# One token tile of head 0 scored ahead in an expert-retrieval layer, and two modulation steps moved

## What is computed

```
mod = silu(c) @ w_ada + b_ada                      # 2048 x 12288: sh1, sc1, g1, sh2, sc2, g2
h   = rmsnorm(x) * (1 + sc1) + sh1
sq, sk, sv, cq, ckv, kr = split(h @ w_in)
sb  = stick_breaking_attention(sq, sk, sv)         # 8 heads of 128
q   = rmsnorm(cq) @ w_uq ; kv = rmsnorm(ckv) @ w_ukv   # latents; rope on 64 columns of each head
x   = x + g1 * (concat(rmsnorm(sb), rmsnorm(mla(q, kv))) @ w_o)
h2  = rmsnorm(x) * (1 + sc2) + sh2
q   = h2 @ w_peer_q                                # 8 heads of 2 halves of 128
s1, s2 = q[..., 0, :] @ keys1, q[..., 1, :] @ keys2
16 best of s1, of s2, and of their 256 sums  ->  16 experts and gates for each token and head
y   = sum over 128 experts of gate * gelu(h2 . u[expert]) * v[expert]
out = rmsnorm(x + g2 * y)
```

## Time and profile before

| | |
|---|---|
| median of three runs | 1845.99 us |
| profiled execution | 1844.33 us |
| its span (first to last instruction) | 1841.7 us |
| DMA over the span | 716 MB, 389 GB/s in the mean |
| granted TensorE clock, mean | 0.972 |
| TensorE, VectorE, ScalarE, GpSimd busy | 80%, 62%, 19%, 34% |
| chain that ended last | DMA 58%, VectorE 15%, TensorE 15%, GpSimd 6% |

### The profile page before, as it was taken

How to read it: one execution, slowest core, us unless ns; L and a number is a source line. 1 busy time by engine, 2 the same in 40 slices (tenths; PEclk the granted TensorE clock), 3 DMA queues, 4 the chain that set the end, 5 groups by cost and what they waited for, 6 DMA issues and landing times.

```text
span 1841.7 us, 13707 instructions
## 1 busy us (share of the span) xinstructions
PE 1475.1 (80%) x4834; PEld 828.1 (45%) x4834; DVE 1142.5 (62%) x1562; ACT 350.9 (19%) x697; POOL 620.3 (34%) x625
## 2 busy tenths in 40 slices
PE   2979998899899897777777777777877777777776
PEld 2549986777788633232323323233322323232332
DVE  5858886688789955555555555538555555544445
ACT  3004332663301211010011101101111111010100
POOL 0001111001154773444343443417643443433341
PEclk9889999999999899999999999998999999999999
DMA  9999998459879999999999999999999999999995
GB/s 341 386 389 404 399 354 326 176 187 379 323 303 413 421 421 421 422 422 422 422 421 422 422 422 422 422 421 402 422 422 422 422 422 421 422 422 422 422 422 233
DMA packets 138241, 716.43 MB, mean 389 GB/s; under 512 B 11158, under 2 KB 15436, under 8 KB 63692
## 3 DMA queue, kind: packets, MB, share of 16 engines
q0 software_dynamic: 82976, 604.02, 79.4%
q1 hardware_dynamic: 55212, 111.77, 16.5%
HBM read 713.65 MB, written 2.10 MB: 389 GB/s over the span
## 4 chain that ended last, share of the span: by engine, by line
DMA 58%; DVE 15%; PE 15%; POOL 6%; issue 4%; ACT 1%; SPq 1%; DVEq 0%; POOLq 0%; ACTq 0%
DMA u_rows<-in_peer_u,expert 49%; DVE u_rows L1740 6%; PE ps L768 4%; DMA v_rows<-in_peer_v,expert 4%; DVE first_acc L454 3%; POOL v_rows L665 3%; POOL u_rows L665 3%; PE ps L762 2%; DMA ada_first<-in_w_ada 2%; PE ps L425 2%; DMA ada_late<-in_w_ada 2%; PE ps L927 2%; DVE ada_acc L293 2%; DMA u_rows<-in_peer_v,expert 1%; PE ps L732 1%
## 5 line engine op out<-in xcount | busy, mean ns | idle before, releaser
L1012 PE MATMUL ps<-v_rows,diag 128*128 128x512 f32 x1960 | 905.6, 608 | 269.8 <-DMA v_rows<-in_peer_v,expert 255.6
L1740 DVE SCALAR_TENSOR_TENSOR u_rows<-u_rows,h 128x2048 f32<-128x2048 f32 x256 | 587.1, 2293 | 519.5 <-DMA u_rows<-in_peer_u,expert 514.7
L1012 PEld LDWEIGHTS ps<-v_rows,diag 128*128 128x128 f32 x1960 | 358.8, 191 | 815.2 <-issue 586.5
L665 POOL DMA_INDIRECT u_rows<-in_peer_u,expert x256 | 284.9, 1113 | 621.1 <-DVE u_rows L1740 576.4
L665 POOL DMA_INDIRECT v_rows<-in_peer_v,expert x249 | 287.2, 1153 | 97.0 <-issue 78.6
L1339 ACT ACTIVATE diag<-ident,hidden 128x128 f32<-128x128 f32 x250 | 89.6, 398 | 847.8 <-PE ps L1012 534.2
L293 DVE SCALAR_TENSOR_TENSOR ada_acc<-ada_late,cact,ada_acc 128x2048 f32<-128x2048 f32 x57 | 133.9, 2349 | 19.5 <-DMA ada_late<-in_w_ada 18.5
L279 POOL DMA_DIRECT2D ada_late<-in_w_ada x61 | 32.4, 532 | 321.9 <-DVE ada_acc L293 275.8
L981 PE MATMUL ps<-h2T,ring 128*128 128x256 f32 x512 | 117.7, 390 | 6.4 <-DMA ring<-in_w_peer_q 6.4
L981 PEld LDWEIGHTS ps<-h2T,ring 128*128 128x128 f32 x512 | 99.6, 197 | 20.6 <-DMA ring<-in_w_peer_q 6.8
L454 DVE SCALAR_TENSOR_TENSOR first_acc<-ada_first,cact,first_acc 128x1024 f32<-128x1024 f32 x60 | 77.0, 1284 | 16.9 <-DMA ada_first<-in_w_ada 11.5
(11 more groups left out here) (273 smaller groups left out, 1256.4 us busy)
## 6 DMA issues: line engine op xcount, KB each, us to landing
ada_late<-in_w_ada POOLq DMA_DIRECT2D x61, 1024.0 KB, 7.7
ada_first<-in_w_ada SPq DMA_DIRECT2D x64, 512.0 KB, 11.7
ring<-in_w_in SPq DMA_DIRECT2D x10, 2048.0 KB, 23.5
ring<-in_w_o SPq DMA_DIRECT2D x8, 2048.0 KB, 19.1
ring<-in_w_peer_q SPq DMA_DIRECT2D x8, 2048.0 KB, 14.3
opened<-in_w_in SPq DMA_DIRECT2D x8, 1024.0 KB, 13.0
u_rows<-in_peer_u,expert POOLq DMA_INDIRECT x256, 32.2
v_rows<-in_peer_v,expert POOLq DMA_INDIRECT x249, 34.2
```

The source lines that it names most:

```text
L665: nc.gpsimd.indirect_dma_start(buf[:, :], None, table, bass.IndirectOffsetOnAxis(ap=expert[:, q, k:k + 1], axis=0)).then_inc(done, 16)
L1012: ins = nc.tensor.matmul(ps[:, c, :], diag[i % len(diag)][:, :], buf[:, 512 * c:512 * c + 512], start=(n % HALF_SLOTS == 0), stop=last)
L1740: nc.vector.scalar_tensor_tensor(out=buf[:, :], in0=buf[:, :], scalar=1.0, in1=h2[:, q // H, :], op0=ALU.mult, op1=ALU.mult, accum_out=hid ...
```

## The change

Three edits. First, head 0 is computed with exchanged operands: `h2T` of one token tile is stationary and the head's 256 weight columns move, tile 0 first, and tile 1 behind it in three pieces. The result has tokens on partitions, so it is copied (`q0`), transposed (`p0_t`), copied into `pq`, scored against the keys of head 0 (`sc0_t`) and copied into `s_all`, each for one tile. `retrieve` waits for the scores of its own tile. Second, `ADA_IN` and `ADA_OUT` go from 71 and 86 to 73 and 88: pieces 71 and 72 are summed ahead of attention, and five instead of seven stand behind the norm. `ada_cols(3)` moves ahead of `qpe`, and `ada_finish(3)` with pieces 64 and 65 ahead of the rope. Third, in the output projection `ada_cols(4)` goes from pair (2,5) to (2,1), and two of the 15 places of pieces change.

```diff
     assert e_next[0] + 512 * len(diag) <= 229376
+    q0 = at("q0", e_next[0], [P, TT, 2 * P])
...
-    plan([f"p{u}" for u in range(8)], [0, 1, 2, 3])
-    plan([f"sc{u}" for u in range(8)], [4, 5])
+    plan(["fq_0", "fq_1", "p0_0", "p0_1"] + [f"p{u}" for u in range(1, 8)], [0, 1, 2, 3])
+    plan(["sc0_0", "sc0_1"] + [f"sc{u}" for u in range(1, 8)], [4, 5])
...
-    ADA_IN, ADA_OUT = 71, 86
+    ADA_IN, ADA_OUT = 73, 88
...
                 fill(ins, f"uq{u}")
+            ada_cols(3)
             wr = w.rearrange("p kc (h n) -> p kc h n", h=H)
...
-            ada_cols(3)
             w = group(pe, "w_ukv", 2 * n_in, KVR // P)
...
-                    if n == 2 and m == 5:
+                    if n == 2 and m == 1:
                         ada_cols(4)
...
+            w0 = ring[item["w_pq0"][0]][:, :].rearrange("p (kc n) -> p kc n", kc=KC)
+            def first_head(t, lo, hi):
+                if lo == 0:
+                    take(pe, f"fq_{t}")
+                for ch in range(lo, hi):
+                    if t == 0 and ch % 2 == 0:
+                        copied(pe, f"h2T{ch // 2}")
+                    if t == 0 and ch % KH == 0:
+                        loaded(pe, "w_pq0", ch // KH)
+                    ins = nc.tensor.matmul(ps[:, unit[f"fq_{t}"][0], 0:2 * P], h2T[:, ch, P * t:P * t + P], w0[:, ch, 0:2 * P],
+                                           start=(ch == 0), stop=(ch == KC - 1))
+                if hi == KC:
+                    fill(ins, f"fq_{t}")
+            def first_turned(t):
+                copied(pe, f"fq_{t}")
+                bank = take(pe, f"p0_{t}")
+                for s in range(2):
+                    ins = nc.tensor.transpose(bank[:, P * s:P * s + P], q0[:, t, P * s:P * s + P], ident[:, :])
+                fill(ins, f"p0_{t}")
+            def first_score(t):
+                copied(pe, f"p0_{t}")
+                bank = take(pe, f"sc0_{t}")
+                for s in range(2):
+                    ins = nc.tensor.matmul(bank[:, P * s:P * s + P], pq[:, 0, s, P * t:P * t + P], kT[:, H * s, :], start=True, stop=True)
+                fill(ins, f"sc0_{t}")
+            first_head(0, 0, KC)
+            first_head(1, 0, 3)
+            first_turned(0)
+            first_head(1, 3, 6)
+            first_score(0)
+            first_head(1, 6, KC)
+            token_rows(0)
+            first_turned(1)
+            token_rows(1)
+            first_score(1)
+            token_rows(2)
+            token_rows(3)
-            for u in range(H):
+            for u in range(1, H):
...
-                if u == 0:
-                    token_rows(0)
-                    score(0)
-                    for k in range(1, 4):
-                        token_rows(k)
...
+            first_query(0)
+            first_query_turned(0)
+            first_scores_out(0)
+            first_query(1)
+            token_rows_out(0)
+            first_query_turned(1)
+            token_rows_out(1)
+            first_scores_out(1)
+            token_rows_out(2)
+            token_rows_out(3)
...
             ada_sums(59, 64)
+            ada_finish(3)
+            ada_sums(64, 66)
             for t in range(TT):
                 bank = full(dve, f"qpe{t}").rearrange("p (h n) -> p h n", h=H)
...
-            ada_finish(3)
-            ada_sums(64, ADA_IN)
+            ada_sums(66, ADA_IN)
...
-                    if (n, m) in ((1, 0), (1, 1), (1, 2), (1, 3), (1, 6), (1, 7), (2, 0), (2, 1), (2, 2), (2, 6), (2, 7), (3, 0), (3, 1), (3, 2), (3, 3)):
+                    if (n, m) in ((1, 0), (1, 1), (1, 2), (1, 3), (1, 6), (1, 7), (2, 0), (2, 3), (2, 6), (2, 7), (3, 0), (3, 1), (3, 2), (3, 3), (3, 4)):
                         ada_sum(next(ada))
...
-                if part == 0 and t == 0:
-                    copied(dve, f"sc{h}")
+                if part == 0 and (t == 0 or h == 0):
+                    copied(dve, f"sc{h}" if h else f"sc0_{t}")
```

More of the change, by code:

```diff
@@ L968, in token_rows @@
                 fill(ins, f"h2_{u}")
-            for u in range(H):
+            w0 = ring[item["w_pq0"][0]][:, :].rearrange("p (kc n) -> p kc n", kc=KC)
[36 more added lines that the diff above has]
+            for u in range(1, H):
                 name, bank = f"w_pq{u // 2}", take(pe, f"p{u}")
                 for m in range(PAIRS):
-                    if u == 0:
-                        copied(pe, f"h2T{m}")
                     if u % 2 == 0 and m % (PAIRS // 2) == 0:
@@ L1267, in query @@
                 if u >= 2:
-                    full(act, f"sc{u - 2}")
+                    full(act, f"sc{u - 2}" if u > 2 else "sc0_1")
                 empty(nc.scalar.copy(pq[:, u % 2, :, :].rearrange("p s t -> p (s t)"), b), f"p{u}")
@@ L1298, in std, with first_query, first_query_turned, first_scores_out @@
                 nc.scalar.activation(st[:, 2 + t:3 + t], st[:, 2 + t:3 + t], ACT.Sqrt).then_inc(y_std, 1)
-            for u in range(H):
+            def first_query(t):
+                empty(nc.scalar.copy(q0[:, t, :], full(act, f"fq_{t}")[:, 0:2 * P]), f"fq_{t}")
+            def first_query_turned(t):
+                empty(nc.scalar.copy(pq[:, 0, :, P * t:P * t + P], full(act, f"p0_{t}")[:, 0:2 * P].rearrange("p (s t) -> p s t", s=2)),
+                      f"p0_{t}")
+            def first_scores_out(t):
+                empty(nc.scalar.copy(s_all[:, t, 0:2, :], full(act, f"sc0_{t}")[:, 0:2 * P].rearrange("p (s n) -> p s n", s=2)),
+                      f"sc0_{t}")
+            first_query(0)
[8 more added lines that the diff above has]
+            token_rows_out(3)
+            for u in range(1, H):
                 if u == 4:
@@ L1304, in _ @@
                 query(u)
-                if u == 0:
-                    token_rows_out(0)
                 scores_out(u)
-                if u == 0:
-                    for k in range(1, 4):
-                        token_rows_out(k)
                 if u == 4:
```

## The result

The median went from 1845.59 us (1843.55 to 1848.41, 9 runs) to **1850.99 us** (1849.27 to 1855.22, 9 runs). The ratio is 1.0033, interval 1.0022 to 1.0043: slower by 5.4 us, where +2.9 and 1848.1 were forecast. The time lies in the range. A later comparison on another chip gave 1.0037 (1.0024 to 1.0050). The profiled execution of the changed kernel took 1850.99 with a span of 1849.3, 7.6 more than the span of before.

What follows compares the result with a forecast made beforehand. The prediction took the transfer stream of expert rows to set the end, its start hanging on a chain from the latents to the first gather. 5.1 - 1.0 - 1.2 = +2.9 us on 1845.2 gave 1848.1 us, range 1840.5 to 1853.5.

Steps and rivals of the forecast that it cites:

- the likeliest outcome: Whole kernel: a time between 1842.3 and 1849.7 us, not told from no change, was given 0.50.
- A: Latents: two more steps ahead of attention start it at 318.55 instead of 313.44, +5.1 us, bounds 2.8 and 7.8.
- attention's length: Attention: a relay between VectorE and ScalarE that absorbs none of the late start; no change of length was priced.
- B: Output projection, VectorE the bound: moved product and pieces remove load waits, -1.0 us, bounds -2.35 and 0.
- C: Head 0 and last pieces: first gather 6.15 us sooner against the chain, cut by the stream to a lead of 1.2.
- the wait for piece 63: Latents: TensorE waits 1.0 us for this piece before the column product moved ahead of qpe.
- the low clock on qpe: Latents: clock 0.50 behind the column product falls on qpe instead of kn, costing 1.9 us there.
- my first rival: Latents: piece 72's load queues behind 4 MB of output weights and takes 8.1 us; shift 5.6, 1850.8 us; chance 0.20.
- four of four: Each of the four column products in the kernel before was followed by a stretch at granted clock 0.50.
- the four cases: Output projection: late load or not, low clock or not, giving -0.3, -1.2, -1.35 and -2.35 us.
- The low clock that I had charged with 1.7: Output projection: behind a 2.8 us TensorE wait between (3,4) and (3,5), slow clock costs 1.7 us on the last three pairs.
- The stream: Expert-row retrieval: transfers set the end, weights start the flow at 518.2, so the lead of 6.15 us shrinks to 1.2.

Runs made afterwards that it cites:

- lat_order: Changed kernel with the column product back behind qpe and all nine pieces 64 to 72 behind the rope, ahead of attention; 1850.72 us, ratio 1.0034.
- warm_gap: Changed kernel with seven matmuls of 512 columns, result unread, ahead of attention's first matmul on the scores; 1849.23 us, ratio 1.0023.
- after: The changed kernel, with all three edits, against the kernel before; 1850.99 us, ratio 1.0033.
- after_again: The changed kernel run once more, unchanged, on another chip; 1851.90 us, ratio 1.0037 to the kernel before.
- steps_only: Changed kernel with the old head 0, so only the modulation steps and column products are moved; 1853.70 us, ratio 1.0042.
- before: The kernel without the change; 1845.59 us.
- late_top16: Kernel before, with pieces 93 to 95 summed ahead of the top 16 of head 0 instead of behind it; 1846.93 us, ratio 1.0011.
- head0_only: Kernel before with the new head 0 and nothing else, pieces and column products where they were; 1845.54 us, ratio 1.0000.
- spare_old_head: spare_slot with the old head 0; 1843.43 us, ratio 0.9988 to the kernel before.
- early_product: spare_slot with the output projection's column product behind pair (1,7) instead of (2,1); 1843.27 us, ratio 0.9990 to the kernel before.
- eighteen: spare_slot with one piece more in the output projection, its column product behind pair (2,0), one piece less ahead of the top 16; 1840.35 us, ratio 0.9976.
- spare_slot: Changed kernel with the latents as before and pieces 71 and 72 at the start of the output projection; 1842.95 us, ratio 0.9989 to the kernel before.

## Why the prediction was right, and where its sum was off

The range held, and so did the sign of the shift. But the likeliest outcome was to be no measurable change (0.50), and it became slower by 0.33%, which had been given 0.33; the shift was about twice the forecast. Means of siblings from the table against the terms of the sum (lat_order has other latents and is left out of the first row, warm_gap of the rest):

| term | forecast | measured | from |
|---|---|---|---|
| A, attention's start | +5.1 | +7.7 | 320.85 (after, after_again, steps_only, warm_gap) less 313.11 (before, late_top16, head0_only) |
| attention's length | 0 | +1.7 | 61.06 (after, after_again, lat_order, steps_only) less 59.35 |
| B, projection | -1.0 | -0.7 | 110.77 (the same four) less 111.47 |
| C with the stream | -1.2 | -1.9 | 33.71 (the same four) less 35.57 |
| sum | +2.9 | +6.8 | medians: +5.4 and +6.9 |

**A was mis-sized.** Each step happened: the wait for piece 63, the low clock on qpe, nine pieces' work that ends late, attention straight behind it. The sizes were off. In the profiled execution the product took 4.56 us and not 3.5 (4.20 to 4.78 in the four kernels with this order), qpe lost 2.6 to the low clock and not 1.9, and piece 63 ended 0.8 later (285.66 against 284.89). So the seven pieces behind the rope began at 302.39 and not at 299.9. From there to attention it took 18.2 us, where I had 18.65: the last load, issued at 312.90, took 5.4 and not 5.7. In the three siblings that stretch took 19.1 to 20.3, because loads that I had at 5.2 us took up to 7.2. The measured median of 1850.99 is that of my first rival (1850.8) almost to the digit, but its load of 8.1 us was not there (5.4 here, 6.1 to 7.1 in the siblings); it showed in lat_order (8.4). A time that fits is no proof of a cause. The low clock behind a product, of which I wrote four of four, is not certain either: over all executions it came behind 41 of 52 products, and behind all four of the ones moved ahead of qpe.

Two sums of the forecast don't come out. VectorE's waits in B are 7.0 before and 5.9 or 4.9 after, a gain of 1.1 or 2.1, where the four cases use 1.35 and 2.35. And A with a last load of 8.1 us is 7.5 (310.4 + 8.1 + 2.45 less 313.44), not 7.8. Both are small against what A missed.

**The term that was missing** is attention's length, which I put at nothing with the sentence "I let none of A be absorbed". I asked whether attention could win time back and not whether it could lose some. TensorE is through with its first scores at 316.8, VectorE is held by pieces until 320.7, and so TensorE stands still for 6.70 us. Its clock is at 0.50 behind that in all executions with such a wait (after, after_again, lat_order, steps_only: waits of 6.70 to 11.54 us, first head 6.74 or 6.75 us), and with the wait filled the first head is 5.45 again. The relay of VectorE, ScalarE and TensorE did not hide the slower matmuls: 1.3 us. The rest of the 1.7 in the table is luck: over all eight kernels with seven pieces ahead of attention its mean length is 60.02 and not 59.35, and the second head took 6.06 to 7.68 us with either. The row with the clock at 0.50 behind a wait of 2.64 stood in the earlier trace rows, and I used it for B only.

**B was right within the noise, and its picture for a part of the stretch.** The wait at piece 80 is 4.88 (forecast 4.9) and the late load 0.84 (forecast 1.0). In the kernel before, the chain that ended last runs over VectorE and its loads from 392.94 to the pair at 431.62, as I had it. In the changed kernel it runs over TensorE, which goes from pair to pair in 2.72 us without a wait, until the product is done, and only then over VectorE and its loads (start us, us, what):

```profile
394.07 43.56 PE ps L928 x192
437.63 3.48 PE ps L305 x32
442.41 1.22 DVE ring_low L421
```

So VectorE's wait for the product was no loss in itself. The -0.7 of the table is not resolved: the three projections before differ by 1.7 us among themselves, and TensorE's waits in them sum to 3.9 us in the mean, against 4.0 in the four after. The low clock that I had charged with 1.7 came in three of nine executions, two of the four in the table among them, and the projections with it are 1.6 us longer in the mean (111.67 against 110.09). In the profiled execution it did not come: TensorE waited 2.42 us at 477.01 and the window behind it was at full clock.

```profile
478.00:480.00 2.00, 2.00 (x9) 1.32 (x8) 1.97 (x3) 0.84 (x2) 0.00 (x0) 1.00 1.05 387
```

The Trainium skill, page "TensorE: Matmul & The Clock Gate", section "HAM oscillation", tells of a kernel whose matmul bursts are parted by waits for data, and in which the clock falls in each wait, so that every burst starts at low clock. The traces here agree for the long waits: behind those of 6.70 to 11.54 us the clock was at 0.50 in four of four. They show it behind shorter ones too, but not each time: three of nine at 2.4 us, and at 3.07, attention's first wait in the kernels with seven pieces, the first head took 5.46 or 5.47 us in six executions and 6.58 and 6.76 in two.

**C was right.** From the norm to the first gather 6.2 us less (forecast 6.15), the scores 3.9 us ahead of the top 16 (forecast 3.1), gather 6 still covered: its release at 546.26 stands where DMA moves 404 GB/s and more. What each part of C is worth I had not said. head0_only and spare_old_head say it: the new head 0 brings the gather 1.9 to 2.9 us forward with five pieces ahead of the top 16 and 0.3 with seven, and the onset in no case by more than 0.3.

**The stream** was the right question: late_top16, steps_only and spare_old_head each moved the first gather alone, by 6.0, 1.9 and 2.9 us, and none moved the onset later. Its rule can be read from the table. With seven pieces left it begins 3.5 to 4.0 us behind the issue of the third query weights, with five 1.7 to 2.1 (early_product: 2.5); in eighteen, where the first gather starts 4.6 us ahead of that issue, it begins 5.0 us behind the gather. That is why C's 6.2 us shrank to 1.9: the weights hang on TensorE, and their issue came no sooner behind the norm (31.9 us on average in both groups). All that was won is the hole behind the weights in the earlier trace rows, which rows now fill.

## What to carry to other kernels

Work that is off the bound is to be put where its engine has slack. An engine's wait is only a hint of slack: the chain that ended last says which engine is late there, and work put into the wait shows it (two pieces at pair (0,4) and one at (2,3) cost nothing). Ahead of a chain of short steps between engines a late step costs its own time, and where TensorE idles for it, some of TensorE's clock (here 7.7 us and about 1.3). And where the end is a stream of transfers, find the event that starts it (here a weight load, not the gather) before pricing what is saved upstream.

## What the runs showed of the hardware

- Low clock came and went between executions of the same instructions: head 2 of attention took 6.06 to 6.08 us in five executions and 7.16 to 7.17, or 7.67 to 7.68, in eight; where it was long, windows at 0.50 stood beside it. That is 1.1 to 1.6 us, more than some edits here were worth.
- Between the pairs (3,4) and (3,5) of the projection, behind a wait of 2.4 us, it fell in three of nine executions, which cost 1.6 us in the mean.
- Behind a column product (32 records of one moving column) the clock fell to 0.50 in 41 of 52 cases, though in 47 of the 52 TensorE had not stood still ahead of it. The product took 3.63 us in most cases, and 4.20 to 4.78 in the five where TensorE had waited 0.7 to 1.1 us for it.
- A load of 1 MB took 5.4 to 7.1 us when it was issued 0.3 to 1.0 us ahead of the first output weights (5.4 at 0.68 in the changed kernel), and the first one issued behind them took 7.7 to 8.9 (8.4 at 1.14 in lat_order).
- The first gather of a stream is slow to start. In eighteen it starts on POOL at 513.79, nothing moves in the window from 516 to 517, and 131 GB/s in 517 to 518. In spare_slot the plain weight load is issued at 513.19, nothing moves in 513 to 514, and 47 GB/s in 514 to 515. By the onset the stream begins 5.0 us behind the one, and 1.7 to 2.5 behind the other.
